# Moving the operand of FFN 2 by 32 bytes in SBUF, in a diffusion-backbone layer on one core

## What the kernel must compute

```python
h  = h  + 0.5 * gate * swiglu(modulate(rmsnorm(h),  ...), ffn_w_in[0], ffn_w_out[0])   # FFN 1, latent
hc = hc + 0.5 * gate * swiglu(modulate(rmsnorm(hc), ...), ffn_w_in[0], ffn_w_out[0])   # FFN 1, context
# w_in projection, pooling group and gated DeltaNet group, w_out   (the mixer)
h  = h  + 0.5 * gate * swiglu(modulate(rmsnorm(h),  ...), ffn_w_in[1], ffn_w_out[1])   # FFN 2, latent only
return rmsnorm(h, final_g)

def swiglu(u, w_in, w_out):
    gate, up = jnp.split(u @ w_in, 2, axis=-1)          # 2048 -> 2 x 5632
    return (jax.nn.silu(gate) * up) @ w_out             # 5632 -> 2048
```

## The kernel before

| tensor | bytes from `xh` | remainder by 128 |
|---|---|---|
| `xh`, `yh` | 0 | 0 |
| `xl`, `x2h` | 32768 | 0 |
| `yl` / `x2l` | 16384 / 49152 | 0 |
| `h_lat`, `raw` | 65536, 81920 | 0 |
| `wh`, `wl` | 98304, 114688 | 0 |
| `hth`, `htl` (row of a block: 2048 bytes) | 167584, 175776 | 32 |
| `wba` / `wbah` / `wbal` (row of a block: 128 bytes) | 183968 / 186016 / 188064 | 32 |

## Time and profile before

### The profile page before, as it was taken

One profiled execution on the slowest core, in us unless ns is written; L12 is line 12 of the kernel. 1 busy time (PEld: TensorE's weight loads), 2 busy tenths in 40 slices (PEclk: granted clock), 3 DMA queues, 4 the chain that ended last, 5 costly groups with the idle time before them and its releaser, 6 DMA issues. The chain is left out here.

```text
span 3021.4 us, 47714 instructions
## 1 busy us (share of the span) xinstructions
PE 2918.0 (97%) x18176; PEld 2540.2 (84%) x18176; DVE 1682.5 (56%) x2465; ACT 964.4 (32%) x1434; POOL 235.0 (8%) x390
## 2 busy tenths in 40 slices
PE   6899999999999999999998999988999999999998
PEld 3677888888888888888887888868889999999998
DVE  2522447475665757475636666745665555555555
ACT  2211222222221222222224455533344433434343
POOL 3000000000000000000002013463120000000001
PEclk9999999999999999999999999989999999999999
DMA  9754245445454857667533466684445565556564
GB/s 361 273 192 164 91 134 172 148 153 165 140 172 152 265 173 245 203 206 243 159 94 84 133 192 189 186 249 151 155 148 181 179 187 183 180 183 185 181 188 132
DMA packets 399049, 541.62 MB, mean 179 GB/s; under 512 B 51024, under 2 KB 301904, under 8 KB 390240
## 3 DMA queue, kind: packets, MB, share of 16 engines
q1 hardware_dynamic: 377264, 434.20, 46.2%
q10 hardware_dynamic: 21680, 106.03, 10.8%
HBM read 518.08 MB, written 22.05 MB: 179 GB/s over the span
## 5 line engine op out<-in xcount | busy, mean ns | idle before, releaser
L1605 DVE TENSOR_TENSOR wl<-raw,wh 128x1024 fp32r<-128x1024 f32 x640 | 782.5, 1232 | 800.7 <-ACT wh L1257 798.6
L1257 ACT CAST wh<-raw 128x1024 fp32r<-128x1024 f32 x640 | 666.7, 1048 | 1578.8 <-PE ps L690 1197.1
L688 PE MATMUL ps<-xh,wh 128*128 128x512 f32 (+1 forms) x1920 | 735.4, 383 | 17.1 <-issue 11.3
L690 PE MATMUL ps<-xh,wl 128*128 128x512 f32 (+1 forms) x1920 | 726.0, 378 | 0.0
L689 PE MATMUL ps<-xl,wh 128*128 128x512 f32 (+1 forms) x1920 | 725.7, 378 | 0.0
L688 PE MATMUL ps<-hth,wh 128*128 128x512 f32 (+1 forms) x1408 | 476.3, 338 | 0.7 <-DVE wl L1605 0.6
L689 PE MATMUL ps<-htl,wh 128*128 128x512 f32 (+1 forms) x1408 | 476.0, 338 | 0.0
L690 PE MATMUL ps<-hth,wl 128*128 128x512 f32 (+1 forms) x1408 | 476.0, 338 | 0.0
L688 PEld LDWEIGHTS ps<-xh,wh 128*128 128x128 f32 x1920 | 364.6, 190 | 89.5 <-issue 17.0
L690 PEld LDWEIGHTS ps<-xh,wl 128*128 128x128 f32 x1920 | 363.7, 189 | 68.2
L689 PEld LDWEIGHTS ps<-xl,wh 128*128 128x128 f32 x1920 | 364.4, 190 | 65.4
(11 more groups left out here) (245 smaller groups left out, 2349.6 us busy)
## 6 DMA issues: line engine op xcount, KB each, us to landing
raw<-in_ffn_w_in SPq DMA_DIRECT2D x704, 256.0 KB, 3.2
raw<-in_ffn_w_out SPq DMA_DIRECT2D x176, 512.0 KB, 4.2
abuf<-in_w_ada ACTq DMA_DIRECT2D x64, 1024.0 KB, 5.9
ada_t<-in_ada SPq DMA_DIRECT2D x64, 512.0 KB, 9.3
abuf<-in_w_ada ACTq DMA_DIRECT2D x64, 512.0 KB, 3.8
raw<-in_w_in SPq DMA_DIRECT2D x128, 256.0 KB, 3.4
gate_t<-in_ada SPq DMA_DIRECT2D x32, 512.0 KB, 5.2
raw<-in_w_out SPq DMA_DIRECT2D x32, 512.0 KB, 4.3
```

The lines of the kernel that those rows point to most:

```text
L688: mm(out, ah, bh, start=first, stop=False)
L690: return mm(out, al, bh, start=False, stop=last)
L1257: nc.scalar.copy(wh[:, t % HL, :], raw[:, t % RAW, :]).then_inc(hi_done, 1)
L1605: tt(wl[:, t % HL, :], raw[:, t % RAW, :], wh[:, t % HL, :].bitcast(F32), ALU.subtract).then_inc(lo_done, 1)
```

## The change

Two tensors that nothing reads or writes are declared around `x2h` and `x2l`. One of 8 float32 (32 bytes) lies ahead of them, one of 24 float32 (96 bytes) behind.

```diff
         with ExitStack() as pooling:
             pg = sb("pg", [P, 2, 4, SEQ], stack=pooling)
             wp = sb("wp", [P, 4, 2, POOL_GROUP], stack=pooling)
+
+        sb("shift_x2", [P, 8])
         x2h = sb("x2h", [P, KT, SEQ], F32R)
         x2l = sb("x2l", [P, KT, SEQ], F32R)
+        sb("shift_back", [P, 24])
         XH, XLO = (xh, x2h), (xl, x2l)
         h_lat = sb("h_lat", [P, KT, SEQ])
```

## The result

The changed kernel took 3033.53 us in the median of 7 runs (3028.34 to 3043.83), against 3021.89 us before (3020.27 to 3024.4, 7 runs of the same comparison). The ratio is 1.0043, with a 95% interval of 1.0026 to 1.0059. It is slower, by 11.6 us between the medians, where -10.5 us was forecast. The profiled execution took 3031.58 us with a span of 3029.8 us, 8.4 us more than before.

What follows compares the result with a forecast made beforehand. TensorE's matmul spacing was taken to bound FFN 2. The up half's -10.5 us, with every other part at 0, took the median from 3021.91 to 3011.4 us (-0.35%), range 3006 to 3022.5 us.

Steps and rivals of the forecast that it cites:

- What bounds the kernel: FFN 2 takes as long as TensorE's matmuls from start to start; only that spacing can move the end.
- Part 1: FFN 2 up half: x2h, x2l at remainder 32 run at the down half's rate, 117.34 for 119.95 ns; -10.5 us.
- Part 2: First eight tiles of group 0 in FFN 2: quicker matmuls mostly wait longer for x2l; 0, at most 0.5 us.
- Part 3: FFN 2: ScalarE, VectorE and the loads keep up with the quicker tiles; cost 0, ScalarE's wait near 360 us.
- Part 4: x2h, x2l writers and tensors from h_lat on, moved by 128 bytes, keep their rates, FFN 1 included; cost 0.
- Slower, through the 128 bytes: FFN 1: xh-to-wh distance goes from 0 to 128 modulo 256, costing up to 30.0 us; 3041.4 us, chance 0.09.
- The row taken as evidence against 256: wbah steps 128 bytes per block, xh 2048, yet three matmuls of either block take the same, 0.70 and 0.69 us.
- No change: Up half's excess comes from something else, such as hth's row step or region; 3021.9 us, chance 0.14.
- Faster by more: FFN 2 up matmuls reach 115 ns, as the streams' state depends on its start; -20.0 us, 3001.9 us, chance 0.05.

Runs made afterwards that it cites:

- x2_only: Kernel before with only x2h and x2l moved, 96 bytes earlier over the dead end of yl (distance 160 from the weights modulo 256); 3013.68 us, ratio 0.9977.
- x2_160_hth_0: Kernel before with x2h, x2l at distance 160 and hth, htl at distance 0 from the weights, the rest unmoved; 3001.91 us, ratio 0.9930.
- rest_128: Kernel before with x2h unmoved and 128 bytes of padding behind x2l, moving everything from h_lat on; 3036.96 us, ratio 1.0057.
- x2_at_192: Kernel before with x2h, x2l alone 64 bytes earlier (distance 192), hth staying at 160; 3002.72 us, ratio 0.9942.
- bench_inherit: Matmul streams alone, no kernel work, each distance run behind each other distance; at 256 columns, distance 160 took 117.3 or 118.6 ns a matmul.
- all_128: Kernel before with 128 bytes of padding ahead of xh, so all tensors move together and every distance stays; 3018.0 us, ratio 0.9991.
- the bench: Matmul streams alone, no kernel work, moving tensors in 32-byte steps against fixed weights; 226.8 to 234.3 ns at 512 columns, 117.3 to 120.0 at 256.
- both_192: Kernel before with x2h, x2l at distance 192, and the hidden activation at 0 in FFN 1 and 192 in FFN 2; 2969.83 us, ratio 0.9844.
- up_192_down_32: As both_192, but in FFN 2 the hidden activation lies 32 bytes into its rows (distance 32); 2976.57 us, ratio 0.9850 against the kernel before.

## Why the prediction was wrong

**What bounds the kernel** was right. In all profiles the matmuls of FFN 1 and FFN 2 moved by their spacing alone. What lies outside varies from execution to execution whatever the kernel: over the 15 profiles of whole kernels the opening, up to the first down half, took 308 to 312 us, and the stretch from the last down half of FFN 1 to the output projection 608 to 617 us. So a few us between two medians say nothing of the rates, and the seams do.

**Part 1**, x2h at the down half's rate: right. 45.06 us an up half was forecast and measured, and FFN 2 gained 10.2 us against 10.5. It was right with less ground than it seemed, and in part by luck. x2_only and x2_160_hth_0 have the same distance and run at 118.67 ns, where the gain of an up half is half as large. What picks the rate at distance 160 stays open. What ran before seems to have a say (rest_128, x2_at_192, bench_inherit), but the distance of the stream before doesn't decide by itself (x2_160_hth_0, and the stream at 160 behind 96 in bench_inherit).

**Part 2** was right: the up half of group 0 took 2314.50 - 2261.89 = 52.6 us. **Part 3** was right: in the same 680 us of FFN 2, which begin 18.6 us later, ScalarE still waited 361.3 us for TensorE, and no wait of TensorE on another engine shows up there.

**Part 4** is the step that failed: "In FFN 1 xh stays and wh moves by 128, remainder still 0 against 0. Cost 0". The remainder has to be taken by 256, and it went from 0 to 128. rest_128 alone brings FFN 1 to the rate of the changed kernel, and all_128 and x2_only leave it at the old one. The cost in FFN 1 was 18.3 us where the sum had 0. With part 1 and 0.3 us of the other stretches that makes the +8.4 us of the two profiles. The prediction had it as a rival at a chance of 0.09: "Slower, through the 128 bytes". Its mechanism was right, and its size, 30.0 us at most, was not reached: 5.5 ns a matmul at distance 128 and not hth's 7.1, and less in the first five tiles of a group.

The period of 128 was never seen. The rows of before had two distances, 0 and 160, which can't tell 128 from 256. The row taken as evidence against 256 could not speak. xh lies at distances 96 and 224 from wbah in turn, and the bench, with weights of 128 columns, gives 233.4 and 233.3 ns for these two at 512 columns. That is 0.3 ns apart in three matmuls, where the row is rounded to 10 ns. The range went as far as "no change", because this evidence had pushed the slower case out.

**No change**, the first rival, fell too. Neither hth's row step nor its region is needed: x2h, with rows of 1024 bytes, ran at 117.34 ns in the changed kernel. The prediction took the 16-byte lines of this rival from the Trainium skill, Advanced Engine Details and Errata, section SBUF Cachelines. Steps of 32 bytes all begin on such a line, and yet the rates differ from step to step. **Faster by more** fell as well: no stream at distance 160 ran below 117.3 ns. The Trainium skill, SBUF — State Buffer, section A bandwidth-pool intuition that's wrong (but worth ruling out), gives TensorE a second, independent read port for the weights. Taken to mean that the place of the weights does not touch the moving stream, it does not fit: rest_128 moved the weights against an unmoved xh and the matmuls went from 227.2 to 232.7 ns. How the two reads meet inside the chip no run here shows.

Also open is the spread of the changed kernel, 3028 to 3044 us, against 3020 to 3024 for the kernel before in the same comparison. Both profiles of it show the 117.3 ns rate. A longer mode at 118.7 ns would fit its upper end but was not caught.

## What to carry over

A pad that "keeps the alignment" is an experiment on every stream whose two operands it moves apart. List the pairs that TensorE reads together, with their distance before and after, and take the period from a measurement. When a matmul stream is slower than its columns explain, read start to start at the seams and try the distances. Here a few paddings and an offset, with the instruction counts unchanged, made 1.5%. Judge a placement by several executions and not by its fastest: the two modes of both_192 lie 28 us apart, while the five times of up_192_down_32 lie within 8 us, though it uses two distances (192 and 32) that have two rates each.

## What the runs showed of the hardware

- The time of a float32r matmul in a dense stream depends on the distance between moving tensor and weights, modulo 256 bytes: 226.7 to 234.3 ns at 512 columns, 113.3 to 120.0 ns at 256, and 111.1 to 111.7 ns at 128, where it hardly matters. The order of the distances changes with the columns.
- At some distances the stream has two stable rates (113.4 and 117.8 ns at 192, 117.3 and 118.7 at 160, both with 256 columns), kept over hundreds of matmuls. What picks one is open. Neither the distance does by itself, nor that of the stream before. The two groups of times of both_192 suggest that it can differ from execution to execution; no profile shows that.
- What the other engines do hardly enters: the bench, where nothing else runs, gives the same rates within 0.1 ns at 256 columns and within 0.7 ns at 512 (233.4 against 232.7 at distance 128).
- The Trainium skill, TensorE: Matmul & The Clock Gate, section Back-to-back issue gap, gives for a matmul by itself, without its weight load, the columns over 2.4 GHz plus 2.5 ns. Worked out from that, as an estimate, it is 109.2 ns at 256 columns and 215.8 at 512. For a stream of weight loads and matmuls the section gives about 131 ns at 512 columns. The best rates seen here, in such streams, are 113.3 and 226.7 ns, so with float32r no distance in steps of 32 bytes reached the first, and none came near the second.
